# Final LayerNorm in two passes: all tokens without the last two expert blocks, then the rows of those blocks

## The reference

```python
def grouped_moe(x, ...):            # each token: the best group, two experts of its four
    ...
    xs = x_pad[slot_tok].reshape(n_blocks, M, D)
    a, g = jnp.split(xb @ w_up[e], 2, axis=-1)
    y = (jax.nn.silu(g) * a) @ w_down[e]
    out = jax.ops.segment_sum(ys * slot_gate[:, None], slot_tok, num_segments=T + 1)[:T]

m = grouped_moe(x, w_router, b_router, w_up[l], w_down[l])
x = layer_norm(DEEPNORM_ALPHA * x + m, ln2_g[l], ln2_b[l])
```

## Time and profile before

| | us |
|---|---|
| median of 3 runs | 1672.71 (1670.56 to 1674.26) |
| the profiled execution | 1670.44 |
| its span, first to last instruction | 1668.8 |
| mean granted TensorE clock | 0.976 of full speed |
| PE busy | 1591.1 (95%) |
| DVE busy | 1175.2 (70%) |
| last matmul of the last expert block ends | about 1632 |
| first tile of `zin` has landed | about 1644 |
| last instruction of DVE ends | about 1665.6 |

### The profile page before, as it was taken

One profiled execution on the slowest core, in us unless ns is written; L12 is line 12 of the kernel. 1 busy time (PEld: TensorE's weight loads), 2 busy tenths in 40 slices (PEclk: granted clock), 3 DMA queues, 4 the chain that ended last, 5 costly groups with the idle time before them and its releaser, 6 DMA issues.

```text
span 1668.8 us, 20227 instructions
## 1 busy us (share of the span) xinstructions
PE 1591.1 (95%) x7701; PEld 1321.2 (79%) x7701; DVE 1175.2 (70%) x1472; ACT 845.0 (51%) x1174; POOL 186.0 (11%) x219
## 2 busy tenths in 40 slices
PE   7999999999999999999999996999999999999991
PEld 6788888888888888888788885788888888887770
DVE  3755868495666666332575666799999999988884
ACT  3113121214556555325221333688888888887773
POOL 0000000202212220000000001111111111111120
PEclk9999999999999999999999996999999999999995
DMA  5144524645232331411553566899999999999966
GB/s 160 39 82 73 127 71 85 79 73 158 82 110 66 109 88 58 145 47 48 171 173 126 173 219 232 334 363 381 370 359 360 354 352 353 347 346 364 355 240 216
DMA packets 156985, 329.29 MB, mean 197 GB/s; under 512 B 15919, under 2 KB 85551, under 8 KB 156890
## 3 DMA queue, kind: packets, MB, share of 16 engines
q1 hardware_dynamic: 140746, 289.69, 53.5%
q0 software_dynamic: 16144, 38.32, 7.7%
HBM read 296.74 MB, written 48.52 MB: 207 GB/s over the span
## 4 chain that ended last, share of the span: by engine, by line
PE 86%; DMA 7%; DVE 4%; issue 1%; SPq 1%; ACT 1%; DVEq 0%; POOLq 0%; ACTq 0%
PE ps L753 53%; PE ps L1050 24%; DMA e_raw<-in_w_down 4%; PE ps L854 2%; PE ps L839 2%; DVE e_lo L1862 2%; PE ps L1057 1%; DMA e_raw<-in_w_up 1%; PE ps L998 1%; DMA x_raw<-in_x 1%; DVE zout L1922 1%; PE ps L1063 1%; SPq L547 1%; DVE zout L1915 1%; PE ps L986 0%
## 5 line engine op out<-in xcount | busy, mean ns | idle before, releaser
L1862 DVE TENSOR_TENSOR e_lo<-e_raw,e_hi 128x1024 fp32r<-128x1024 f32 x376 | 435.7, 1219 | 26.2 <-ACT e_hi L1358 22.3
L1358 ACT ACTIVATE e_hi<-e_raw 128x1024 fp32r<-128x1024 f32 x376 | 368.1, 1050 | 28.7 <-DMA e_raw<-in_w_down 21.7
L753 PE MATMUL ps<-xt_hi,w_hi 128*128 128x512 f32 x896 | 303.3, 395 | 2.4 <-DVE xt_lo L1461 2.4
L753 PE MATMUL ps<-xt_lo,w_hi 128*128 128x512 f32 x896 | 299.1, 390 | 0.0
L753 PE MATMUL ps<-xt_hi,w_lo 128*128 128x512 f32 x896 | 298.7, 390 | 0.0
L753 PEld LDWEIGHTS ps<-xt_hi,w_lo 128*128 128x128 f32 x896 | 168.5, 188 | 36.0
L753 PEld LDWEIGHTS ps<-xt_hi,w_hi 128*128 128x128 f32 x896 | 168.3, 188 | 35.1 <-DVE xt_lo L1461 2.6
L753 PEld LDWEIGHTS ps<-xt_lo,w_hi 128*128 128x128 f32 x896 | 168.8, 188 | 33.1
L1494 DVE TENSOR_TENSOR w_lo<-w_raw,w_hi 128x512 fp32r<-128x512 f32 x136 | 94.8, 703 | 129.7 <-ACT w_hi L1127 126.3
L1127 ACT ACTIVATE w_hi<-w_raw 128x512 fp32r<-128x512 f32 x136 | 83.6, 628 | 200.4 <-PE ps L753 199.6
L1050 PE MATMUL ps<-e_hi,xe_hi 128*128 128x512 f32 x512 | 164.6, 403 | 10.9 <-DVE e_lo L1862 8.6
(11 more groups left out here) (278 smaller groups left out, 2251.4 us busy)
## 6 DMA issues: line engine op xcount, KB each, us to landing
e_raw<-in_w_up SPq DMA_DIRECT2D x128, 1024.0 KB, 21.9
e_raw<-in_w_down SPq DMA_DIRECT2D x64, 1024.0 KB, 21.7
w_raw<-in_w_in SPq DMA_DIRECT2D x64, 256.0 KB, 4.9
w_raw<-in_w_gate SPq DMA_DIRECT2D x48, 256.0 KB, 3.5
gates_d<-gate_t POOLq DMA_DIRECT2D x16, 512.0 KB, 3.5
gate_s<-gates_d SPq DMA_DIRECT2D x16, 512.0 KB, 3.6
qkv_d<-qkv POOLq DMA_DIRECT2D x12, 512.0 KB, 3.6
w_raw<-in_w_branch SPq DMA_DIRECT2D x24, 256.0 KB, 3.8
```

The lines of the kernel that those rows point to most:

```text
L753: last = nc.tensor.matmul(o(h, c1 - c0), st(k), mv(k, c0, c1), start=start and k == nk[0] and n == 0, stop=h in stop and k == nk[-1] and n ...
L1358: nc.scalar.activation(e_hi[:, (UPT + s) % RSPL, :], e_raw[r][:, s % 2, :], ACT.Copy).then_inc(e_h, 1)
L1862: nc.vector.tensor_tensor(e_lo[:, sp_, :], e_raw[raw_slot(b, s)][:, s % 2, :], e_hi[:, sp_, :], ALU.subtract).then_inc(e_all, 1)
```

## The change

`LATE = 2` names the blocks that are left to a second pass: block 30 (its index in the tables is `tail + 1`) and block 31 (`tail + 2`).

- SP waits with `ye_out` for the scatters of blocks 0 to 29 alone, and then loads the 8 tiles of `z_d`. It reads `tail` for this. SP stores the 8 tiles as before.
- POOL, behind the scatter of block 29, copies the row numbers of blocks 30 and 31 into `row_l`. It waits until all 8 loads of `zin` have landed, then scatters block 30 (with addition), waits for it, and gathers the rows of block 30 and those of block 31 from `z_d` into `zlate` [128 x 2 x 1025].
- ACT writes block 31's result into its own tile `ye_last`, after the statistics of tile 3 and ahead of those of tile 4. The load of the table for the root is now ahead of it. Behind tile 7 ACT does two more tiles, t = 8 and 9, from `zlate`.
- DVE adds `ye_last` to `zlate[:, 1]` behind the first 8 first passes, and does two more tiles into `zlate_out`. Block 31's rows are not scattered to `z_d` any more.
- POOL waits until all 8 stores of `out` have landed, then scatters `zlate_out` to `out` (a plain write, 1024 wide): block 30's rows, and when these have landed, block 31's. A token in both blocks is wrong in `zlate[:, 0]` and right in `zlate[:, 1]`, which is written last.
- `zin` moves by 0.25 KB, `zout` becomes eight tiles at free places of their own, `zsq` and `zst` move.

PE's program is the same.

```diff
+LATE = 2
-            sp.wait_ge(ye_out, 16 * (last_b + 1))
+            sp.wait_ge(e_all, item(STATIC, 0))
+            tail = nc.sync.value_load(tail_i[0:1, 0:1], min_val=NE - 3, max_val=NBLK - 3)
+            sp.wait_ge(ye_out, 16 * (tail + 1))
             for t in range(TT):
                 sp.dma_start(zin[:, t, :], z_d[t * P:(t + 1) * P, :]).then_inc(tile_in[t], 16)
...
-            for k in range(3):
-                scatter(tail + 1 + k)
+            scatter(tail + 1)
+            for i in range(LATE):
+                pool.wait_ge(row_ok, tail + 1 + i)
+                pool.sem_inc(passed, 1)
+                nc.gpsimd.tensor_copy(row_l[:, i:i + 1], tok_tab[:, bass.ds(tail + 1 + i, 1)]).then_inc(row_ok, 1)
+            pool.wait_ge(row_ok, tail + 1 + LATE)
+            for t in range(TT):
+                pool.wait_ge(tile_in[t], 32)
+            pool.wait_ge(ye_ok, tail + 3)
+            pool.sem_inc(passed, 1)
+            nc.gpsimd.indirect_dma_start(out=z_d, out_offset=bass.IndirectOffsetOnAxis(ap=row_l[:, 0:1], axis=0),
+                                         in_=ye[:], in_offset=None, compute_op=ALU.add,
+                                         bounds_check=SEQ - 1, oob_is_err=False).then_inc(ye_out, 16)
+            pool.wait_ge(ye_out, 16 * (tail + 2))
+            pool.sem_inc(passed, 1)
+            for i in range(LATE):
+                nc.gpsimd.indirect_dma_start(out=zlate[:, i, :], out_offset=None, in_=z_d,
+                                             in_offset=bass.IndirectOffsetOnAxis(ap=row_l[:, i:i + 1], axis=0),
+                                             bounds_check=SEQ - 1, oob_is_err=False).then_inc(late_in, 16)
+            for u in range(4):
+                pool.wait_ge(out_dma[u], 16 * TT // 4)
+            for i in range(LATE):
+                pool.wait_ge(out_ok, TT + 1 + i)
+                if i:
+                    pool.wait_ge(late_out, 16 * i)
+                nc.gpsimd.indirect_dma_start(out=out[0], out_offset=bass.IndirectOffsetOnAxis(ap=row_l[:, i:i + 1], axis=0),
+                                             in_=zlate_out[:, i, :], in_offset=None,
+                                             bounds_check=SEQ - 1, oob_is_err=False).then_inc(late_out, 16)
+            pool.wait_ge(late_out, 16 * LATE)
...
-            result(tail + 3, UPT, 0)
-
             nc.scalar.activation(zst[:, 0, 5:6], eps[:], ACT.Sqrt)
...
+            for t in range(TT + LATE):
+                if t == KC:
+                    result(tail + 3, UPT, 0, ye_last)
+                z, st = z_tile(t), zst[:, t, :]
+                if t < TT:
+                    act.wait_ge(tile_in[t], 32)
+                else:
+                    act.wait_ge(late_in, 16 * LATE)
+                if t == TT + LATE - 1:
+                    act.wait_ge(ln9, 2 * TT)
...
-            for t in range(TT + 1):
-                if t < TT:
+            for t in range(TT + LATE + 1):
+                if t == TT:
+                    dve.wait_ge(late_in, 16 * LATE)
+                    dve.wait_ge(ye_ok, last_b + 2)
+                    dve.sem_inc(passed, 1)
+                    nc.vector.tensor_tensor(zlate[:, 1, :], zlate[:, 1, :], ye_last[:], ALU.add).then_inc(ln9, 1)
+                if t < TT + LATE:
                     dve.wait_ge(z_mean, t + 1)
```

More of the change, by code:

```diff
@@ L261, in program @@
         x1_scaled = at("x1_scaled", [P, D], FP32, 76)
[L262 to L265, removed]
+        zin = at("zin", [P, TT, D + 1], FP32, 79.75)
+        zlate = at("zlate", [P, LATE, D + 1], FP32, 160)
+        zlate_out = at("zlate_out", [P, LATE, D], FP32, 176)
+        zout = [at(f"zout{i}", [P, D], FP32, kb) for i, kb in enumerate((184, 188, 192, 196, 132, 136, 64, 68))]
+        ye_last = at("ye_last", [P, D + 1], FP32, 169)
+        zsq = at("zsq", [P, D], FP32, 140)
+        zst = at("zst", [P, TT + LATE, 16], FP32, 202)
         lng2 = at("lng2", [P, D], FP32, 124)
@@ L351, in program, with z_tile, z_out @@
             assert raw_count(STATIC, _s) == STATIC - RTURN
+        def z_tile(t):
+            return zin[:, t, :] if t < TT else zlate[:, t - TT, :]
+        def z_out(t):
+            return zout[t][:] if t < TT else zlate_out[:, t - TT, :]
         def ntiles(r):
@@ L1370, in split_h, with result @@
                 nc.scalar.activation(ht_hi[:], tiles(6, 1), ACT.Copy).then_inc(ht_h, 1)
-            def result(b1, extra=0, bank=2):
+            def result(b1, extra=0, bank=2, dst=ye):
                 act.wait_ge(e_used, UPT + b1 * XT + RSPL - extra)
-                if not isinstance(b1, int) or b1 > 1:
+                if dst is ye and (not isinstance(b1, int) or b1 > 1):
                     act.wait_ge(ye_out, 16 * (b1 - 1))
-                nc.scalar.activation(ye[:, 0:D], flat(bank), ACT.Copy, scale=gate_tab[:, bass.ds(b1 - 1, 1)],
-                                     accum_out=ye[:, D:D + 1]).then_inc(ye_ok, 1)
+                nc.scalar.activation(dst[:, 0:D], flat(bank), ACT.Copy, scale=gate_tab[:, bass.ds(b1 - 1, 1)],
+                                     accum_out=dst[:, D:D + 1]).then_inc(ye_ok, 1)
             def step(b):
@@ L1411, in _ @@
             result(tail + 2)
-            result(tail + 3, UPT, 0)
             nc.scalar.activation(zst[:, 0, 5:6], eps[:], ACT.Sqrt)
[L1417 to L1420, removed]
+            for t in range(TT + LATE):
[8 more added lines that the diff above has]
+                    act.wait_ge(ln9, 2 * TT)
+                nc.scalar.activation(st[:, 1:2], z[:, D:D + 1], ACT.Copy, scale=-1.0 / D).then_inc(z_mean, 1)
                 act.wait_ge(z_mean, t + 1)
-                nc.scalar.activation(zsq[:], zin[:, t, 0:D], ACT.Square, bias=st[:, 1:2], accum_out=st[:, 2:3]).then_inc(z_var, 1)
+                nc.scalar.activation(zsq[:], z[:, 0:D], ACT.Square, bias=st[:, 1:2], accum_out=st[:, 2:3]).then_inc(z_var, 1)
                 act.wait_ge(z_var, t + 1)
```

12 lines of the change are left out of this document (8 added, 4 removed).

## The result

| | kernel before | changed kernel |
|---|---|---|
| median, 9 runs each | 1672.43 us (1670.56 to 1674.26) | 1676.89 us (1676.19 to 1678.85) |
| ratio, with its 95% interval | | 1.0027 [1.0018, 1.0035] |
| span of the profiled execution | 1668.8 us | 1675.3 us |

The change costs 4.5 us, where 5.9 us less had been forecast. The page shows little of it: the chain's shares by engine are those of before to within two points.

A forecast was written before the change was run, and what follows sets the result against it. Bound taken: the serial tail from 1624.8, DVE idle 20 us, then pacing 21.2 us. Terms summed to 1652.6 + 1.0 + 4.4 + 4.4 + 0.5 = 1662.9 against 1668.8, 5.9 us less: 1666.8 us, range 1662.0 to 1673.1.

The forecast's parts named there:

- the last one of the sum: Program's end: the span ends 0.5 us after the last write lands, 1662.4 + 0.5 = 1662.9.
- four rivals: Alternative outcomes: 1663.0 (0.24), 1673.1 (0.18), 1680.6 (0.05), and loads held until PE's end, 1680.1 (0.01).
- The third: POOL's chain, zin's end to last write: transfers each lose a 1.28 us DVE pass, dear writes; 1680.6 us, chance 0.05.
- Part 1: Loads of zin on SP: start early, at 1616.1, all landed at 1632.0, between 1629.2 and 1633.2.
- Part 2: Eight tiles beside PE's last block: DVE's first pass at 1625.75, not 1644.40; DVE ready for late rows at 1645.6.
- Part 3: POOL's added transfers: scatter 7.0 us to 1639.1, gathers 7.0 to 1646.1 (1639.3 to 1653.6); DVE waits 0.5 us.
- Part 4: Second pass and last stores: addition 1.2 us, tile 7 stored at 1652.6, two writes of 4.4 us, end of writes 1662.4.
- 1.0 us for a DVE pass: Ahead of the first write to out: POOL's work held by a DVE pass, 1.0 us in the sum.
- The first: Tail: DVE stays the bound, late rows there by 1645.6, indirect writes cheap at 3.2 us; 1663.0 us, chance 0.24.
- The second: POOL's chain at loaded prices: scatter 9.9 us, gathers 9.3, DVE waits 6.8; 1673.1 us, chance 0.18.

The follow-up runs named there:

- a_own_copy: Changed kernel with block 30's scatter and the two gathers on a separate HBM buffer, without POOL's wait for the zin loads; 1671.96 us, ratio 1.0000.
- b_pool8: Kernel before with one wait added, holding POOL's program until the last tile of out is normalized; 1677.46 us, ratio 1.0038.
- a_sp_waits: Changed kernel with the wait for the last two indirect writes moved from POOL to SP; 1675.09 us, ratio 1.0019.
- a_own_sp_par: a_own_copy with the last wait on SP and both indirect writes issued back to back, block 31's to another buffer; 1666.86 us, ratio 0.9972.

## Why the prediction was wrong

The steps are set against the changed kernel's trace with 1.1 us taken off, so that the scatter of block 29 stands where it stood before.

| step | predicted | measured, less 1.1 | from the step itself |
|---|---|---|---|
| loads of `zin` issued | 1616.1 | 1616.4 | +0.3 |
| DVE's first pass | 1625.75 | 1625.5 | |
| last load landed (1620.92 + 13.0) | 1632.0 | 1632.8 | +0.5 |
| block 30's scatter landed (1635.10 + 7.3) | 1639.1 | 1641.3 | +1.4 |
| both gathers landed | 1646.1 | 1650.0 | +1.7 |
| tile 7's store landed | 1652.6 | 1656.7 | +0.2 |
| last write landed | 1662.4 | 1665.3 | -1.2 |
| span's end | 1662.9 | 1674.2 | +8.4 |

**The step that failed is the last one of the sum**: "the span ended 0.5 us later". That 0.5 us was read from a program whose last engine was SP, and carried over to one whose last engine is POOL. There it is 8.9 us, of which the drain on POOL is 8.4. With the 0.5 the kernel would have ended at 1665.8 in the terms of before, 3.0 us less than it; with the 8.9 it is 5.4 more. None of the four rivals had it. The third put a slower result on POOL too, but for another reason, which the trace contradicts (below). The order of the programs showed POOL's program ending on a wait for its own last write; that this was new for POOL asked for a term of its own. Its price stood in the trace of the kernel before, in the view of the program's last line: the drain of 11.0 us above, which ended 9.2 us after POOL's last instruction (1636.1 to 1645.3). With 9.2 in place of 0.5 the sum comes to 1671.6, slower than before.

**Part 1 held.** The loads started where they were put, and the last one landed 0.8 us after the value taken, inside its bounds.

**Part 2 held.** DVE's first pass came 0.25 us earlier than said, block 31's result on ACT delayed nobody, and PE's end did not move against the tail.

**Part 3 came out 3.9 us late**, 0.8 of it handed on by Part 1, and within its bounds (1639.3 to 1653.6). The transfers were priced well: the scatter took 7.3 us for 7.0; the second gather landed 7.8 us after the first one's start for 7.0. What the sum lacked was POOL's way from a landing to the next issue: 1.2 us ahead of the scatter (1633.9 to 1635.10), 0.9 ahead of the gathers (1642.4 to 1643.35), and again 1.0 and 0.9 ahead of the two writes. The chain of the changed kernel has the third of these steps as `issue`, between the landing of the store and the write:

```profile
1655.17 2.60 DMA out<-zout
...
1658.01 0.77 issue
1658.78 3.49 DMA out<-zlate_out,row_l
```

The chain before has such a step too, 0.95 us from the end of ACT's result (1633.57) to the scatter at 1634.52. It was there to be read and stands in no term.

**Part 4** was right in its order, and partly by luck in its sum: the addition took 1.23 us for 1.2, the store 2.60, and a plain indirect write 3.5 and 3.2 us where 4.4 was taken and 3.2 to 6.1 bounded. The value should have been the idle gather's, 3.2. The two writes were thus priced 2.1 us too high, which hid a part of the missing steps. The 1.0 us for a DVE pass ahead of the first write has the size of what stands there, but what stands there is the step from the landing to the issue.

**The rivals.** The first had the cheap writes right and DVE's lead wrong: DVE stalled 4.9 us for `late_in`. The second had a sound mechanism for loaded transfers, which `a_own_copy` shows (9.2 us beside the loads), but in the changed kernel the scatter waits for the loads to be over and so doesn't meet them. The third, POOL held by DVE, was small at most: block 30's scatter took 2.46 us to issue and not 1.58, the first gather 1.46 and the second 1.03, the writes 1.24 and 0.99. Against 1.58, 1.03 and 0.99 that is some 1.6 us in all and not 3.8 to 5, and no run here shows whether DVE was the cause. The lock that the Trainium skill describes (SBUF — State Buffer, "Who interferes with whom") would allow up to one DVE pass for each, and its inference on descriptor writing would allow none; the rows lie between the two (0 to 0.9 us). The Trainium skill's fit of 2.0 us plus the bytes at 436 GB/s for a transfer by GpSimd (DMA: Bandwidth & Descriptors, "Anatomy of one DMA — SWDGE (gpsimd) path") gave an estimate of 2.6 us for such a write; 3.5 us (66 rows) and 3.2 (94 rows) were measured, plus the 0.9 to 1.0 us ahead of each issue.

## What to carry to other kernels

Ask of every change which engine ends last now, and what its end costs: the time from the last landing to the end of the span is a row like any other, and it belongs to the engine that is last. The drains in the view of the program's last line give it even while they are hidden. If GpSimd has issued many transfers and is going to be last, give it a drain earlier, where it is idle. And in a chain of dependent transfers by one engine count the step from each landing to the next issue (here 0.9 to 1.2 us, four times) along with the transfers.

## What the runs showed of the hardware that was not expected

- A drain on GpSimd took 8.2 to 8.8 us behind 106 to 140 of its own transfers, 2.7 us behind 31 more, 0.45 us behind five, and 0.16 us right behind another drain, though all transfers had landed each time. The end of the program holds such a drain, which the timeline doesn't show: 8.19 us in `b_pool8`, 8.44 in the changed kernel.
- With ACT in the same place, ending late cost nothing (tail 62.9 us against 62.6, its drain 8 ns).
- In `a_sp_waits` and `a_own_sp_par`, where POOL didn't wait for its last write, the drain was over 8.45 us after POOL's last instruction, although that write landed only 2.2 to 2.4 us behind the instruction.
- A plain indirect write to HBM landed 3.5 us (66 rows of 4 KB) and 3.2 us (94 rows) after its issue. The scatter with addition took 6 us with idle DMA engines, 7.3 beside stores, and 9.2 beside loads.
